# The odd layer's output product in seven block products per pair, with banks that add up

## What is computed

```python
def odd_layer(x, norm_g, w_in, conv_w, w_out):
    h = rmsnorm_2(x, norm_g)
    z = h @ w_in                       # 1024 -> 14336 columns, taken in 56 pairs of 128-column tiles
    ...                                # three dilated attentions per head, 8 heads -> y_c (1024 channels)
    ...                                # short gated convolution                 -> y_d (1024 channels)
    return x + jnp.concatenate([y_c, y_d], axis=-1) @ w_out      # 2048 -> 1024 channels
...
return rmsnorm_2(h, final_norm)        # after the odd layer; this is the output
```

## Time and profile before

| | |
|---|---|
| median of 3 runs | 3325.83 us (3325.39 to 3329.54) |
| span of the profiled execution (first to last instruction) | 3322.8 us |
| TensorE busy | 3117.1 us, 94% of the span |
| VectorE, ScalarE, GpSimd busy | 1872.1, 1262.8, 1611.1 us |
| odd layer's pairs (1844 to 3127 us) | TensorE busy throughout, but for its start |
| output product and tail of the odd layer | 3127 to 3304 us, and 18.8 us behind it |

### The profile page before, as it was taken

How to read it: one execution, slowest core, us unless ns; L and a number is a source line. 1 busy time by engine, 2 the same in 40 slices (tenths; PEclk the granted TensorE clock), 3 DMA queues, 4 the chain that set the end, 5 groups by cost and what they waited for, 6 DMA issues and landing times. The chain is left out here.

```text
span 3322.8 us, 43242 instructions
## 1 busy us (share of the span) xinstructions
PE 3117.1 (94%) x15972; PEld 2569.3 (77%) x15972; DVE 1872.1 (56%) x2681; ACT 1262.8 (38%) x2142; POOL 1611.1 (48%) x1056
## 2 busy tenths in 40 slices
PE   6978999887799779999999799999999999999999
PEld 4667888765688657788887688888888888888887
DVE  5666623845799585633531756556556555555712
ACT  5256323714477542222300444444344344222311
POOL 2331332043212147867643566556556556688732
PEclk8989999999899889999999899999999999999999
DMA  8230113174699842222431111111111111222331
GB/s 289 54 84 32 44 38 101 38 253 150 244 395 395 294 141 64 79 76 74 133 127 51 53 48 48 55 39 58 45 43 54 48 55 42 80 74 73 118 101 70
DMA packets 312577, 354.00 MB, mean 107 GB/s; under 512 B 28487, under 2 KB 280299, under 8 KB 306100
## 3 DMA queue, kind: packets, MB, share of 16 engines
q1 hardware_dynamic: 301182, 311.36, 27.9%
q0 software_dynamic: 4608, 16.78, 2.0%
q10 hardware_dynamic: 6582, 23.13, 1.8%
HBM read 293.28 MB, written 54.53 MB: 105 GB/s over the span
## 5 line engine op out<-in xcount | busy, mean ns | idle before, releaser
L2695 POOL TENSOR_TENSOR odd_quarter_lo<-odd_w_sums,odd_quarter_hi 128x512 fp32r<-128x512 f32 x224 | 298.6, 1335 | 279.9 <-ACT odd_quarter_hi L2690 278.3
L2730 PE MATMUL first_z<-odd_t_hi,odd_quarter_hi 128*128 128x512 f32 x784 | 327.7, 418 | 18.3 <-DVE odd_t_lo L4184 18.3
L2730 PE MATMUL odd_z<-odd_t_hi,odd_quarter_hi 128*128 128x512 f32 x784 | 326.0, 416 | 0.8 <-POOL odd_quarter_lo L2695 0.8
L2695 POOL TENSOR_TENSOR odd_quarter_lo<-odd_raw,odd_quarter_hi 128x512 fp32r<-128x512 f32 x168 | 229.8, 1368 | 167.2 <-ACT odd_quarter_hi L2690 162.8
L2732 PE MATMUL first_z<-odd_t_hi,odd_quarter_lo 128*128 128x512 f32 x784 | 308.5, 394 | 0.0
L2732 PE MATMUL odd_z<-odd_t_hi,odd_quarter_lo 128*128 128x512 f32 x784 | 307.3, 392 | 0.0
L2731 PE MATMUL first_z<-odd_t_lo,odd_quarter_hi 128*128 128x512 f32 x784 | 307.2, 392 | 0.0
L2731 PE MATMUL odd_z<-odd_t_lo,odd_quarter_hi 128*128 128x512 f32 x784 | 305.9, 390 | 0.0
L2690 ACT CAST odd_quarter_hi<-odd_w_sums 128x512 fp32r<-128x512 f32 x224 | 139.6, 623 | 365.7 <-PE odd_z L2732 178.9
L2746 DVE SCALAR_TENSOR_TENSOR dil_set<-first_z,dil_set 128x512 f32<-128x512 f32 x196 | 170.6, 883 | 143.4 <-PE first_z L2732 138.5
L2746 DVE SCALAR_TENSOR_TENSOR dil_set<-odd_z,dil_set 128x512 f32<-128x512 f32 x196 | 170.7, 884 | 137.0 <-PE odd_z L2732 132.5
(11 more groups left out here) (624 smaller groups left out, 8219.9 us busy)
## 6 DMA issues: line engine op xcount, KB each, us to landing
odd_raw<-in_odd_w_in SPq DMA_DIRECT2D x224, 256.0 KB, 3.4
raw_gate<-in_w_gate SPq DMA_DIRECT2D x16, 2048.0 KB, 16.1
raw_up<-in_w_up SPq DMA_DIRECT2D x16, 2048.0 KB, 15.8
raw_down<-in_w_down SPq DMA_DIRECT2D x16, 2048.0 KB, 15.6
even_raw<-in_even_w_in SPq DMA_DIRECT2D x80, 256.0 KB, 3.4
start_w_mod<-in_w_mod SPq DMA_DIRECT2D x11, 1024.0 KB, 10.8
w_raw<-in_w_in SPq DMA_DIRECT2D x16, 512.0 KB, 3.7
mix_w_early<-in_w_mod SPq DMA_DIRECT2D x8, 1024.0 KB, 11.8
```

Source lines behind the costliest of these rows:

```text
L2695: pool.tensor_tensor(self.w_lo[:, n % self.SLOTS], self.source(m, i), self.w_hi[:, n % self.SLOTS].bitcast(F32), ALU.subtract).then_inc(se ...
L2730: pe.matmul(to, self.w_hi[:, slot, kt], t_hi[:, kt], start=(kt == 0), stop=False)
```

## The change

1. **Shared banks, in both layers.** The seven products are taken in another order (A11, S1, S2, A12, S3, S4, A22 with their token operands), chosen so that products 2, 4 and 6 add up in the bank of product 0 after it has been copied out, and product 5 in that of product 1. A pair uses three banks, the next pair the mirrored three. ScalarE now takes four banks out (products 0, 1, 2, 6) and VectorE three (3, 4, 5).
2. **The output product of the odd layer** becomes pairs 56 to 63 of `Quarters` (`OUT = 56`): the 2048 input channels are two chunks of 1024, with four pairs of output tiles for each. VectorE adds each product's bank in place to `last_x` (`add_up`, one add for each product). The seven token operands must be made anew from `y_cm` for each chunk, in the places of the old ones, while the pair before still runs.
3. The squares, their sums and the last norm are moved: they follow tile by tile in the last chunk, and the second token half is ended first, so that its row blocks go out while the first half is still being finished.
4. In the even layer ScalarE's split of `y` stands before its copy of the last product.

The core of the diff:

```diff
             def multiply(self, pe, m, i, banks, tokens, between=None):
                 n, slot = 7 * m + i, (7 * m + i) % self.SLOTS
                 pe.wait_ge(self.split, n + 1)
-                if n >= self.BANKS:
-                    of, which = (n - self.BANKS) // 7, (n - self.BANKS) % 7
-                    if which == 0:
-                        pe.wait_ge(self.p1_out, of + 1)
-                    else:
-                        pe.wait_ge(self.evicted, 7 * of + self.FREE[which])
-                to = banks[n % self.BANKS]
+                if i == 0 and m >= 2:
+                    self.wait_taken(pe, m - 2, 6)
+                if i == 1 and m:
+                    self.wait_taken(pe, m - 1, 3)
+                if i == 2:
+                    self.wait_taken(pe, m, 0)
+                if i == 3 and m:
+                    self.wait_taken(pe, m - 1, 5)
+                if i == 4:
+                    self.wait_taken(pe, m, 2)
+                if i == 6:
+                    self.wait_taken(pe, m, 4)
+                to, begins = banks[self.bank_of(m, i)], i in (0, 1, 3)
...
+            def bank_of(self, m, i):
+                return ((0, 1, 0, 2, 0, 1, 0), (3, 2, 3, 1, 3, 2, 3))[m % 2][i]
...
+            def add_up(self, dve, m, i, banks, to):
+                t, half = self.PLACES[i]
+                dve.wait_ge(self.product, 7 * m + i + 1)
+                if 7 * (m - self.out) + i:
+                    dve.wait_ge(self.landed, 7 * (m - self.out) + i)
+                dve.tensor_tensor(to[t][half], self.bank(m, i, banks, to), to[t][half], ALU.add).then_inc(self.landed, 1)
...
+            OUT = CONV_AT + CONV_PAIRS
+            PER_CHUNK = KT // 2
+            PAIRS = OUT + 2 * PER_CHUNK
...
+                    def last_t2(chunk):
+                        dve.wait_ge(t_added, 4 * (chunk + 1) + 2)
+                        dve.wait_ge(quarters.product, 7 * last_of(chunk) + T2_SUM + 1)
+                        token_sum(T2_SUM, y22[:], last_raw(chunk, T1_SUM)[:])
...
+                    def last_lo(chunk, i):
+                        dve.wait_ge(t_hi_done, 7 * (chunk + 1) + i + 1)
+                        if i == T2_SUM:
+                            dve.wait_ge(t_added, 4 * (chunk + 1) + 4)
+                        dve.tensor_tensor(odd_tokens[i][1][:], last_raw(chunk, i)[:], odd_tokens[i][0][:].bitcast(F32), ALU.subtract).then_inc(t_lo_done, 1)
...
+                    for m in range(OUT, PAIRS):
+                        chunk = (m - OUT) // PER_CHUNK
+                        fresh, again = m == OUT + PER_CHUNK * chunk, m == last_of(1)
+                        final, late = m == PAIRS - 1, m > OUT + PER_CHUNK
+                        if fresh:
+                            last_t4(chunk)
+                            last_lo(chunk, T2_SUM)
+                        land(m, 0)
+                        if fresh:
+                            last_lo(chunk, B21)
+                        land(m, 1)
...
-                    for k in range(2 * KT):
-                        n, first = unit(k)
-                        u = k % 2
-                        pe.wait_ge(wo_split, k + 1)
...
-                            for w, rhs, begin, end in ((wo_hi, y_hi[c], c == 0, False), (wo_hi, y_lo[c], False, False), (wo_lo, y_hi[c], False, c == KO - 1)):
-                                for b in range(2):
-                                    ins = pe.matmul(z[n % 2][:, b, :], w[:, u, kt], rhs[:, b * HALF:(b + 1) * HALF], start=begin, stop=end)
-                        ins.then_inc(projected, 1)
+                    for m in range(CONV_AT + 2, PAIRS):
+                        for i in range(7):
+                            multiply(m, i, {2: lambda: sum_half(1, KT + 1)} if 7 * m + i == 7 * PAIRS - 1 else None)
```

More of the change, by code:

```diff
@@ L2738, in bank @@
             def bank(self, m, i, banks, to):
-                return to[2](banks[(7 * m + i) % self.BANKS])
-            def p1(self, act, m, banks, to, scale=1.0):
-                act.wait_ge(self.product, 7 * m + 1)
-                act.activation(to[0][0], self.bank(m, 0, banks, to), ACT.Copy, scale=scale).then_inc(self.p1_out, 1)
-            def join(self, dve, product, out, more, scale):
-                dve.scalar_tensor_tensor(out=out, in0=product, scalar=scale, in1=more, op0=ALU.mult, op1=ALU.add).then_inc(self.evicted, 1)
@@ L2774, in c12, with copy @@
-            def c12(self, dve, m, banks, to, scale=1.0):
-                dve.wait_ge(self.product, 7 * m + 7)
-                dve.wait_ge(self.evicted, 7 * m + 5)
-                self.join(dve, self.bank(m, 6, banks, to), to[0][1], to[0][1], scale)
+                return to[2](banks[self.bank_of(m, i)])
+            def copy(self, act, m, i, banks, to, scale=1.0):
+                t, half = self.PLACES[i]
+                act.wait_ge(self.product, 7 * m + i + 1)
+                act.activation(to[t][half], self.bank(m, i, banks, to), ACT.Copy, scale=scale).then_inc(self.copied, 1)
@@ new lines, in join @@
+            def join(self, dve, m, i, banks, to, scale=1.0):
+                t, half = self.PLACES[i]
+                dve.wait_ge(self.product, 7 * m + i + 1)
+                dve.wait_ge(self.copied, 4 * m + self.JOINED[i])
+                dve.scalar_tensor_tensor(out=to[t][half], in0=self.bank(m, i, banks, to), scalar=scale, in1=to[t][half], op0=ALU.mult,
+                                         op1=ALU.add).then_inc(self.joined, 1)
+            def add_up(self, dve, m, i, banks, to):
+                t, half = self.PLACES[i]
+                dve.wait_ge(self.product, 7 * m + i + 1)
+                if 7 * (m - self.out) + i:
+                    dve.wait_ge(self.landed, 7 * (m - self.out) + i)
+                dve.tensor_tensor(to[t][half], self.bank(m, i, banks, to), to[t][half], ALU.add).then_inc(self.landed, 1)
@@ L3688, in targets @@
             def targets(m):
+                if m >= OUT:
+                    n = pair_order[(m - OUT) % PER_CHUNK]
+                    return [[last_x[:, n + t, half] for half in (T1, T2)] for t in range(2)] + [lambda bank: bank]
                 if m >= CONV_AT:
@@ L4145, in _ @@
-                    for half in range(2):
+                            hi(m, 0)
+                            copy(m, 1)
+                            hi(m, 1)
+                            copy(m, 2)
+                            hi(m, 2)
+                            hi(m, 3)
+                            store_y(KT + c - 1, conv_acc)
+                            hi(m, 4)
+                            hi(m, 5)
+                            copy(m, 6)
+                            hi(m, 6)
+                            act.wait_ge(y_done, KT + c)
@@ L4156, in _ @@
+                    root(1, 3)
+                    times_gain(KT - 2, T1, KT + 1)
+                    square(KT - 1, T1, done + 7)
+                    take_rows(0)
+                    times_gain(KT - 1, T1, KT + 2)
+                    take_rows(1)
+                    root(0, 4)
+                    for r in range(2, BLOCKS):
+                        take_rows(r)
                 @block.vector
```

811 lines of the change are left out of this document (408 added, 403 removed).

## The result

The changed kernel takes 3329.91 us (median of 20 runs, 3327.44 to 3334.93), the kernel before 3324.77 us (20 runs, 3323.18 to 3329.54): a ratio of 1.0016 with a 95% interval of 1.001 to 1.0022. That is 5.1 us slower, clear of zero and inside the 0.2% that the prediction had called the same.

The account below looks back on a forecast made before the run. TensorE was taken to be busy practically throughout, so time is matmuls plus interruptions. Terms -24.3 + 26.2 + 1 + 1.5 - 1.5 = +2.9 us gave 3328.7 us beside 3325.8; 8-in-10 range 3304 to 3345 us.

Parts of the forecast that it names:

- Product saves 24.3 us: Odd layer's output product: 672 matmuls in 152.4 us replace 176.7 us, -24.3 us if TensorE never stands.
- Turns on the port cost 26.2 us: Pairs 56, 57, 59, 60: two-SBUF-input VectorE and GpSimd instructions exclude each other; TensorE stands 13.1 us per chunk, +26.2.
- The sign of being right: TensorE waits of 11 to 16 us for `odd_quarter_lo` and `odd_t_lo` around pairs 56 and 57, again around 60 and 61.
- The first wait: Ahead of pair 56's first product, TensorE would wait about 5 us.
- The clock, +1.5 us, mostly hidden: Each chunk's first wait may lower TensorE's clock; slower matmuls mostly hide behind late operands, +1.5 us (0 to +4).
- Shared banks, 0 and +1 us: Less bank slack costs 0; later high casts delay GpSimd in the even layer's group-3 pairs, +1 us (-1 to +2).
- No waits for banks before 3070 us: Sign of the forecast being right: TensorE never waits for a shared bank before 3070 us.
- Rival C: Attention pairs of eight heads: product 4's join comes late, +16 to +24 us, total 3345 to 3353; chance 0.20.
- The tail, -1.5 us: Behind the last matmul: second token half ready early, rows leave at some 3.6 us instead of 6.1; -1.5 us (-3 to 0).
- Sum: Whole kernel: the terms add to +2.9 us, 3328.7 us beside 3325.8 us before.
- Rival B: Output product: token work hides, TensorE stands at most 2 or 3 us per chunk; 3306 us, without stalls 3301; chance 0.20.
- Rival D: Pairs 56, 57, 60, 61: waits keep the clock down, partly unhidden, some 5 us per chunk, 3337 us; chance 0.07.

Follow-up runs that it names:

- run 1: Changed kernel with VectorE's 22 token sums and low parts of the two chunks left out (bare signals instead); 3300.0 us, one run.
- run 2: Changed kernel with GpSimd's weight work left out in pairs 55 to 63, token work whole; 3312.2 us, one run.
- run 3: Changed kernel with each 128x2048 token instruction made four of 128x512 with one input in PSUM, other values; 3318.4 us, one run.
- run 4: Changed kernel with each token instruction cut into four of 128x512, all inputs in SBUF; 3347.1 us, one run.
- run 8: Changed kernel with the gate behind pair 56 and 19 weight low parts made by VectorE instead of GpSimd; 3319.4 us, 0.9983 to the kernel before.
- run 6: Changed kernel with the last two instructions of the convolution's gate moved behind pair 56's last add; 3327.9 us, 1.0003 to the kernel before.
- run 7: Changed kernel with the second token half's sum, and VectorE's mean and inverse, moved behind the last product; 3329.7 us, 1.0013 to the kernel before.
- run 5: Changed kernel with 40 TensorE transposes of a constant ahead of pair 56's first product, where it stood waiting; 3325.0 us.
- run 9: Changed kernel with VectorE's list reordered, 15 weight low parts by VectorE, gate behind pair 56, even layer's copies moved; 3317.3 us, 0.998 to the kernel before.
- run 10: Changed kernel with VectorE's two gate-table copies moved behind the second join of the even layer's first pair; 3329.7 us, one run.

## Why the prediction came out right, step by step

- **Product saves 24.3 us.** Right: 154.9 us with the token work left out, 2.4 of it the sum over channels, so 152.5 for 176.5.
- **Turns on the port cost 26.2 us.** The mechanism is shown by runs 1 to 4 and 8. The adding up of both lists is close: the low part for pair 57 ended 49.8 us behind the start of pair 55 (3163.46 us) where 51.2 was forecast, and pair 61 started 51.5 us behind the start of pair 59, where 51.2 was. The size in us is right only together with the clock's term: 28.7 us measured against 26.2 + 1.5. Its split is not: 18.2 us of waits, some 8 us of low clock, 2.5 us of restarts and short pauses.
- **What TensorE waits for.** The sign of being right named waits for `odd_quarter_lo` and `odd_t_lo`. In fact 10.3 of the 18.2 us are waits for `last_x`, VectorE's adds, which stand behind token work in its list while a shared bank is wanted; 7.9 us are GpSimd's low parts and what the profile calls issue, none is for a token low part by name. In chunk 0 GpSimd's low part for (57,0) was ready 3.3 us before TensorE got there. The first wait was forecast at about 5 us and measured at 4.74. Product (56,6), for which I had 1.5 to 2 us at product 4, waited 5.21 us, because the gate stood ahead of the add of product 4 too; the tenths at each later product in chunk 0 aren't there.
- **The clock, +1.5 us, mostly hidden.** This term failed. Low clock came behind four waits (4.7, 5.2, 2.0 and 3.1 us long) and took some 8 us. Where it was kept away in one place, pair 56 became 3.0 us shorter. That the sum fits is luck: the waits are 8 us less than forecast.
- **Shared banks, 0 and +1 us.** 0.3 us in the odd pairs and +1.5 in the even layer, the same in eight further profiles (680.0 to 680.2 us, and 679.9 in two more with the copies moved). Both places are joins late by one product's slack, and neither is in the group-3 pairs that I had named: pair 0 gives some 0.7 us, and in the layer's last pair product 6 waits 0.71 us for a join (row below), with 0.9 us lost. GpSimd's waits went from 1.2 to 1.5 us. "No waits for banks before 3070 us" so fails in the even layer. Rival C's place, the attention pairs, shows none.

```profile
PE even_z L2761 <- DVE spat_u_cm L2781: 0.7, 1, 0.7
```

- **The tail, -1.5 us.** Measured: -2.0 us behind the last matmul in this profile, but +2.4 us for the sum inside the last product, which I had at 0.5. Together +0.4, so this term is off by 1.9 us.
- **Sum.** +2.9 forecast, +5.1 measured by the medians and +6.6 by the stretches of the profiles. Of the 3.7 us up to the latter, 1.9 are the tail's with the sum in the last product, 1.0 the stalls' and the clock's, 0.5 the even layer's, 0.3 the odd pairs', and -0.1 the product's, with rounding. The time itself, 3328.7 us for 3329.9, came closer than the difference by chance: it was counted from a median of 3325.8 us of three runs, where twenty have 3324.8. The 3.0 us from span to median were of the same three runs; in the changed kernel's profiled execution they are 1.7 us.

Rival B (token work hidden) is what run 1 reaches by leaving the work out; run 3 goes half the way, with 14.9 us where B had at most 5. Rival D was right that low clock costs its own time; its price, 10 us, was near the 8 measured, and it came with shorter waits, not on top of them.

Open: why the tail's transposes ran at the lower clock in the profiles of the changed kernel and of runs 6 and 7, and less or not at all in others. The changed kernel first, then run 3:

```profile
3320.77 1.95 PE L3903 MATMUL odd_z<-const,last_x 128*128 128x128 f32 x8
```

```profile
3305.24 1.07 PE L3903 MATMUL odd_z<-const,last_x 128*128 128x128 f32 x8
```

The tail behind the last matmul's start took 17.2 us in the one and 15.2 us in the other, with the same instructions; it took 15.2 us in runs 1, 2, 4 and 8 too, 16.0 to 16.3 us in runs 5, 9 and 10, and 17.3 us in run 6. So the -2.0 us of the tail above could have been -4.0 with another execution of the changed kernel.

Open too is which waits bring the clock down. One of 2.0 us, ahead of (59,6), was followed by 0.50; one of 2.4 us, ahead of (61,0), was not, nor was one of 3.3 us in run 8, ahead of (60,2). The length of a wait alone doesn't decide it.

## What to carry to other kernels

Before putting VectorE work with two SBUF inputs into a stretch where GpSimd is busy, add the times of both and compare the sum with the stretch; neither engine's own busy share shows it (VectorE was under 60% and GpSimd at 75 to 83% before). What helps is less time on the port: an input out of PSUM, or GpSimd's work done by VectorE in half the time (7.0 us of the stretch here, besides 3.9 us for the gate's place), and not shorter pieces, which only hand turns to the other engine. Where the engine that TensorE waits for can't be made faster, look at each bank's last reader and put it ahead of longer work.

## What the runs showed of the hardware

- Four VectorE instructions of 128x512 with one input in PSUM and one in SBUF, 2.4 us, left GpSimd's at 1.30 us (run 3). With both inputs in SBUF (run 4) GpSimd's took 1.3 to 1.8 us and VectorE's 0.94 to 1.19 us each on average (0.68 us in run 3), so the two engines took turns one by one.
- VectorE's 128x2048 instructions with two inputs in SBUF took 2.28 us with GpSimd's work left out (run 2), and 2.8 to 3.4 us beside it in the changed kernel, where GpSimd's 128x512 instructions took 3.1 to 3.3 us in place of 1.3.
- At the lower clock matmuls of 128x512 started 0.43 us apart, at the higher 0.23. Waits of 2.0, 3.1, 4.7 and 5.2 us were followed by 0.50; one of 2.4 and one of 3.3 us were not.
- 40 transposes of 128x128 in 4.53 us kept the granted clock at 1.00 where it had fallen to 0.50 (run 5).
- The tail of the same instructions took 15.2 us in some profiles, 16.0 to 16.3 and 17.2 to 17.3 us in others; in a profile of the first and one of the last kind the same eight transposes took 1.07 and 1.95 us.
